# A down projection of a feed-forward slab: one more pair of output tiles by seven half-size products instead of eight

## What is computed

```python
D_FF_2 = 2816
def conv_ffn(h, w_up, conv_w, conv_b, w_down):
    u = h @ w_up                      # 1024 -> 2 * 2816
    u = lax.conv_general_dilated(u, conv_w[:, None, :], ...) + conv_b   # 3 taps along the tokens
    a, gate = jnp.split(u, 2, axis=-1)
    return (jax.nn.silu(gate) * a) @ w_down   # 2816 -> 1024
```

## Time and profile before

| | |
|---|---|
| median of 3 runs | 3196.84 us (3196.56 to 3198.14) |
| time of the profiled execution | 3196.49 us |
| its span in the trace | 3194.6 us |
| PE busy | 3179.1 us (100%) |
| DVE, ACT, POOL busy | 2049.5 us (64%), 1298.8 us (41%), 503.0 us (16%) |
| granted TensorE clock | 0.999 |

### The profile page before, as it was taken

How to read it: one execution, slowest core, us unless ns; L and a number is a source line. 1 busy time by engine, 2 the same in 40 slices (tenths; PEclk the granted TensorE clock), 3 DMA queues, 4 the chain that set the end, 5 groups by cost and what they waited for, 6 DMA issues and landing times.

```text
span 3194.6 us, 45570 instructions
## 1 busy us (share of the span) xinstructions
PE 3179.1 (100%) x16502; PEld 2681.1 (84%) x16502; DVE 2049.5 (64%) x2876; ACT 1298.8 (41%) x1758; POOL 503.0 (16%) x436
## 2 busy tenths in 40 slices
PE   9999999999999999999999999999999999999998
PEld 7788888889998788888889998768888888888887
DVE  8455567586557455567586555666877744588776
ACT  4433333334443433333334453354443523554433
POOL 2100000123221100000123221052202101322111
PEclk9999999999999999999999999999999999999999
DMA  7256324423333156324423332203233332122332
GB/s 268 67 167 208 125 93 167 142 93 106 100 105 101 58 165 205 130 92 164 146 91 108 99 102 87 86 21 101 97 106 99 105 99 92 47 79 93 105 99 79
DMA packets 100044, 359.31 MB, mean 112 GB/s; under 512 B 11057, under 2 KB 13361, under 8 KB 99761
## 3 DMA queue, kind: packets, MB, share of 16 engines
q1 hardware_dynamic: 98960, 354.08, 33.6%
q0 software_dynamic: 928, 3.17, 0.3%
HBM read 355.11 MB, written 2.10 MB: 112 GB/s over the span
## 4 chain that ended last, share of the span: by engine, by line
PE 94%; DVE 1%; POOLq 1%; issue 1%; ACT 1%; DMA 1%; DVEq 0%; SPq 0%; ACTq 0%; POOL 0%
PE pb L759 21%; PE pb L761 21%; PE pb L760 21%; PE pb L1074 6%; PE pb L1314 3%; PE pb L829 2%; PE pb L831 2%; PE pb L830 2%; PE pb L791 1%; PE pb L792 1%; PE pb L795 1%; PE pb L1182 1%; PE pb L1613 1%; DMA raw<-stream 1%; PE pb L1615 1%
## 5 line engine op out<-in xcount | busy, mean ns | idle before, releaser
L2348 DVE TENSOR_TENSOR lo<-raw,hi 128x1024 fp32r<-128x1024 f32 (+1 forms) x484 | 601.5, 1249 | 320.6 <-ACT hi L1685 294.8
L1685 ACT ACTIVATE hi<-raw 128x1024 fp32r<-128x1024 f32 x484 | 508.5, 1056 | 730.8 <-PE pb L761 436.3
L759 PE MATMUL pb<-yH,hi 128*128 128x512 f32 (+1 forms) x1664 | 644.7, 387 | 0.0
L760 PE MATMUL pb<-yL,hi 128*128 128x512 f32 (+1 forms) x1664 | 644.5, 387 | 0.0
L761 PE MATMUL pb<-yH,lo 128*128 128x512 f32 (+1 forms) x1664 | 644.4, 387 | 0.0
L759 PE MATMUL pb<-hH,hi 128*128 128x512 f32 x1128 | 440.8, 391 | 0.0
L760 PE MATMUL pb<-hL,hi 128*128 128x512 f32 x1128 | 439.3, 389 | 0.0
L761 PE MATMUL pb<-hH,lo 128*128 128x512 f32 x1128 | 439.2, 389 | 0.0
L761 PEld LDWEIGHTS pb<-yH,lo 128*128 128x128 f32 x1664 | 312.6, 188 | 63.7
L760 PEld LDWEIGHTS pb<-yL,hi 128*128 128x128 f32 x1664 | 312.6, 188 | 63.2
L759 PEld LDWEIGHTS pb<-yH,hi 128*128 128x128 f32 x1664 | 312.7, 188 | 63.0
(11 more groups left out here) (537 smaller groups left out, 5550.1 us busy)
## 6 DMA issues: line engine op xcount, KB each, us to landing
raw<-stream SPq DMA_DIRECT2D x648, 512.0 KB, 3.4
yF<-first SPq DMA_DIRECT2D x8, 512.0 KB, 11.9
act<-first SPq DMA_DIRECT2D x8, 512.0 KB, 16.5
x<-xT SPq DMA_DIRECT2D x4, 512.0 KB, 7.0
outT<-act SPq DMA_DIRECT2D x7, 256.0 KB, 2.2
act<-crow POOLq DMA_DIRECT2D x2, 512.0 KB, 5.4
tab<-decay SPq DMA_DIRECT2D x1, 1024.0 KB, 7.7
scr<-ws POOLq DMA_DIRECT2D x2, 256.0 KB, 3.1
```

The lines of the kernel that those rows point to most:

```text
L759: pe.matmul(out, whi, ahi, start=first, stop=False)
L760: pe.matmul(out, whi, alo, start=False, stop=False)
L1685: act.activation(hi[:, s], raw[:, s], ACT.Copy).then_inc(hi_ready, 1)
L2348: dve.tensor_tensor(lo[:, s, 0:width], raw[:, s, 0:width], hi[:, s, 0:width].bitcast(F32), ALU.subtract).then_inc(lo_ready, 1)
```

## The change

Pair 1 (down tiles 2 and 3) of the four stretches is done by seven products too, so that only tiles 0 and 1 are plain. As tiles 0 and 1 alone stand ahead of pair 1, several steps are cut finer or moved:

- The first weight sum goes to a place of its own (`d_first`, in `act3`) instead of over a21, and is rounded by its own ACT and DVE steps (`down_sum_hi`, `down_one_lo`); `down_hi` and `down_lo` of slot s1 now take only the upper half of the tile. The order of the sums is first, e2, e4, e3.
- In pair 1, e2, e4 and e3 are rounded and subtracted one by one, 512 wide each. `down_sum_lo` of e2 waits until e4 is made, since its output lies over e2.
- t1 of the last token pair is made by POOL (`m_first`) while product 7 is still being made, and rounded and subtracted ahead of `multiplied(n - 1)`; t4 is rounded ahead of t2 and t3.
- PE does the product with t4 (`lower_sum`) ahead of the one with the first sum and t1 (`other_sum`).
- The loads into slots 2 and 3 of the second four down tiles now wait for pair 1's sums.

```diff
-FAST_DOWN, DOWN_GROUPS = (0, 1), (2, 3)
+FAST_DOWN, DOWN_GROUPS = (0, 1), (1, 2, 3)
+        d_first = lambda q: act3[:, q]
@@ POOL: down_sums
-                four_sums(d_tile(layer, j) + 2 * g, [e[:, i] for i in range(3)],
-                          5 * (at - 1))
+                pool.wait_ge(p_full, 5 * (at - 1 if g == 3 else at if g == 1 else at - 2))
+                pool.tensor_tensor(one, a21, a22, ALU.add)
+                pool.drain().then_inc(s1_ready, 1)
+                pool.tensor_tensor(e2, one, a11, ALU.subtract)
...
+                pool.tensor_tensor(e4, a12, e2, ALU.subtract)
...
+                pool.tensor_tensor(e3, a11, a21, ALU.subtract)
+                pool.drain().then_inc(w_sums, 1)
@@ POOL: middle_sums
+                    pool.wait_ge(product, made + KT - 1)
+                    pool.tensor_tensor(t1, b1[:, TH[1]], b1[:, TH[0]], ALU.subtract)
+                    pool.drain().then_inc(m_first, 1)
@@ PE: fast_down
-                for group in (range(3), (3,)):
...
+                for s in range(2):
+                    pe.wait_ge(lo_ready, tiles.next())
+                    pe.wait_ge(bank_free, banks.next())
+                for m in range(KT):
+                    w = slice((m % 2 * 4 + m // 2) * P, (m % 2 * 4 + m // 2 + 1) * P)
+                    pe.wait_ge(y_ready, y0 + m + 1)
+                    for s in range(2):
+                        ins = three(pb[:, s], hi[:, s, w], lo[:, s, w], midH[:, m], midL[:, m], m == 0, m == KT - 1)
@@ PE: down_group
-                if g == DOWN_GROUPS[0]:
+                if g == 1:
+                    pe.wait_ge(m_lo, tokens_made - 1)
+                product_of(lower_sum, own(s1, 1), token(4)).then_inc(p_full, 1)
+                pe.wait_ge(e_lo, e_count(layer, j, g) - (3 if g == 1 else 1))
+                product_of(other_sum, own(s1, 0), token(1)).then_inc(tile_done, 1)
+                if g == 1:
                     pe.wait_ge(m_lo, tokens_made)
-                product_of(other_sum, own(s1, 0), token(1)).then_inc(p_full, 1)
-                product_of(lower_sum, own(s1, 1), token(4)).then_inc(tile_done, 1)
-                pe.wait_ge(e_lo, at + 1)
+                pe.wait_ge(e_lo, e_count(layer, j, g) - (2 if g == 1 else 0))
                 pe.wait_ge(x_part, added + 1)
                 product_of(one_sum, summed_w(2), token(2), False).then_inc(p_full, 1)
@@ ACT: end of a slab
+                    if fast:
+                        down_hi(layer, j, 1, 1)
+                        act.wait_ge(m_first, slab + 1)
+                        middle_hi(3, 0, 1)
                     gate(n - 1)
                     first += n
                     if fast:
                         act.wait_ge(m_last, slab + 1)
-                        middle_hi(3)
-                        tick(0)
+                        middle_hi(3, 3)
+                        middle_hi(3, 1, 3)
+                        down_sum_hi(layer, j, 1)
```

More of the change, by code:

```diff
@@ L310, in build @@
         d_product = lambda layer, j: layer * (sum(SLABS) - len(SLABS)) + sum(SLABS[:j]) - j
+        d_middle = lambda layer, j: 56 * LAYERS + 8 + layer * (sum(SLABS) + 12) + sum(SLABS[:j])
         gain2 = sb("gain2", [P, 8])
@@ L382, in build @@
         m_last = sem("m_last")
+        m_first = sem("m_first")
         m_hi = sem("m_hi")
@@ L1281, in fast_down @@
             def fast_down(layer, j, y0):
-                for group in (range(3), (3,)):
[L1284 to L1293, removed]
+                for s in range(2):
[6 more added lines that the diff above has]
+                        ins = three(pb[:, s], hi[:, s, w], lo[:, s, w], midH[:, m], midL[:, m], m == 0, m == KT - 1)
+                        if m == KT - 1:
+                            ins.then_inc(tile_done, 1)
                 for g in DOWN_GROUPS:
@@ L3014, in other_of @@
                 def other_of():
-                    dve.wait_ge(p_full, p + 2)
+                    dve.wait_ge(tile_done, done.next(2))
                     dve.tensor_tensor(x1[:, TH[1]], Y, x1[:, TH[1]], ALU.add).then_inc(x_part, 1)
@@ L3024, in lower_of @@
                 def lower_of():
-                    dve.wait_ge(tile_done, done.next(2))
+                    dve.wait_ge(p_full, p + 2)
                     dve.tensor_tensor(x1[:, TH[0]], Z, x1[:, TH[0]], ALU.add)
@@ L3047, in fast_down, with plain_add @@
             def fast_down(layer, j):
-                tick(0)
-                middle_lo(layer, j, 3)
-                for k in range(RING):
+                def plain_add(k):
                     drained.next()
@@ L3054, in fast_down @@
                     dve.tensor_tensor(x[:, k], pb[:, k], x[:, k], ALU.add).then_inc(bank_free, 1)
-                    if k in (1, 2):
-                        down_lo(layer, j, 2, k - 1)
+                one, other, two, lower, upper, last = x_adds(layer, j, 1)
+                middle_lo(layer, j, 3, 3)
+                down_one_lo(layer, j, 1)
+                middle_lo(layer, j, 3, 1, 3)
+                plain_add(0)
+                one()
+                down_sum_lo(layer, j, 1, 0)
+                plain_add(1)
+                lower()
+                down_sum_lo(layer, j, 1, 2)
+                other()
+                two()
+                down_sum_lo(layer, j, 1, 1)
+                down_lo(layer, j, 2, 0)
+                upper()
+                down_lo(layer, j, 2, 1)
+                last()
                 one, other, two, lower, upper, last = x_adds(layer, j, 2)
+                down_one_lo(layer, j, 2)
+                one()
                 down_sum_lo(layer, j, 2)
-                one()
+                lower()
+                other()
+                two()
                 down_lo(layer, j, 3, 0)
-                other()
-                lower()
-                two()
+                upper()
                 down_lo(layer, j, 3, 1)
-                upper()
                 last()
@@ L3068, in fast_down @@
                 one()
+                down_one_lo(layer, j, 3)
                 down_sum_lo(layer, j, 3)
+                lower()
                 tick(1)
                 other()
-                lower()
                 two()
@@ L3134, in conv_ffn @@
                             ins.then_inc(conv_done, 1)
+                    if fast:
+                        down_lo(layer, j, 1, 1)
+                        middle_lo(layer, j, 3, 0, 1)
                     multiplied(n - 1)
```

77 lines of the change are left out of this document (56 added, 21 removed).

## The result

The changed kernel takes 3201.38 us (median of 22 runs, 3200.88 to 3202.37), the kernel before 3196.89 us beside it (22 runs, 3196.33 to 3198.14): a ratio of 1.0014, 95% interval 1.0008 to 1.0021. It is slower by 4.5 us. That is less than the 0.2% (6.4 us) that I had set as the bound of what can be told, but the interval lies wholly above 1, so with this many runs the slowdown is clear of the noise. The profiled execution took 3201.63 us, its span is 3199.9 us, 5.3 more than before. The forecast was 3202.0 and +5.1.

The account below looks back on a forecast made before the run. PE was taken to bound the kernel, busy 3179.1 of 3194.6 us. Waits of 8.3 us less 3.2 saved gave +5.1: 3201.6 profiled, 3202.0 median; overall range 3193.4 to 3207, the main forecast's own 3198 to 3207.

Parts of the forecast that it names:

- PE's gain, a stretch: PE's work per stretch: a pair takes 10.08 us by seven products against 10.88 plain, saving 0.80 us.
- POOL's t1 on DVE: End of the up part: POOL making t1 stretches DVE's work by 0.6 us, bounds 0 and 0.74.
- last product begins: DVE, end of the up part: last product starts 6.9 us after the first plain matmul, instead of 6.11.
- last product published: End of the up part: last product split and published at 9.05 us, in time for PE's need at 9.52.
- rest of e2 ends: Pair 1 on DVE: ends at 17.4 us, held up by POOL's last sum, wanted at 16.64, so 0.9 late.
- rest of e4 ends: Pair 1 on DVE: ends at 19.15 us, wanted at 18.08 + 0.9, 0.6 late with the product's start-up.
- rest of slot 0 (pair 2) ends: DVE's 1024-wide step for pair 2: ends at 23.1 us, wanted at 22.5, 0.75 late with the start-up.
- waits of the first stretch: PE's four waits in stretch one: 0.9 + 0.6 + 0.75 + 0.45 = 2.7 us.
- second, third, fourth: PE's waits in the later stretches, shifted by when DVE's last product starts: 1.25, 3.1 and 1.25 us.
- Rival 2: POOL's chain of sums gets late for pair 3: 2.5 us more a stretch, +15, 3212 us; 9 in 100.
- all is hidden: Rival 1: PE's waits mostly do not arise, change worth 0 to -3.2 us, 3193.6 to 3196.8; 27 in 100.
- Dearer short products: Rival 3, PE: seven short products cost more than two plain tiles, +19, 3216 us; one in 100.

Follow-up runs that it names:

- e3: Not a run in this text: the last of pair 1's four weight sums made by POOL, forecast to end at 16.85 us after the first plain matmul.
- the kernel with ACT copies: Changed kernel with ACT copies in place of POOL's weight sums for pairs 1 and 2, output wrong: 3193.52 us, ratio to before 0.9989.
- the unused sums: Eight sums nobody reads, put on POOL in the kernel where ACT copies replace pairs 1 and 2's sums: 3198.05 us, ratio to before 1.0003.
- pair 1's sums early: Changed kernel with POOL making pair 1's four weight sums during the up part: 3210.35 us, ratio to before 1.0043.
- pairs 1 and 2 early: Changed kernel with POOL making the weight sums of pairs 1 and 2 during the up part: 3221.45 us, ratio to before 1.0075.

## Why the prediction was right

The sum was +5.1, the stretches gave +4.74, the medians +4.5. That the profiled execution came out within 0.1 us of its forecast (3201.63 against 3201.6) is luck: 0.58 of its +5.14 lies ahead of the first stretch, where the change does nothing. Step by step, times from F in the first stretch:

| step | forecast | measured |
|---|---|---|
| PE's gain, a stretch | 0.80 | 0.81 (41.92 against 41.11, POOL away) |
| POOL's t1 on DVE | 0.6 | 0.58 (1.81 for 1.23) |
| last product begins | 6.9 | 7.03 |
| last product published | 9.05 | 9.00 |
| pair 1's sums end | 16.85 | 16.82 |
| rest of e2 ends | 17.4 | 17.37 |
| rest of e4 ends | 19.15 | 19.07 |
| rest of slot 0 (pair 2) ends | 23.1 | 23.00 |
| pair 2's 1536-wide rest ends | 29.3 | 29.19 |
| waits of the first stretch | 2.7 | 2.62 |
| second, third, fourth | 1.25, 3.1, 1.25 | 1.49, 2.66, 1.14 |

(For "published", 6.9 and the 1.97 that the three steps take in the earlier trace rows make 8.87, not 9.05; the later start made up for the slip.) The mechanism is the one forecast, and the steps of the first stretch lie within 0.15 us of where they were put, from turns read in two pairs of rows and carried through some twenty instructions by hand. Four smaller steps failed.

- *"rest of e4 at 19.15, wanted at 18.08 + 0.9: 0.6 late".* The size is right (0.58) and the releaser wrong. 19.15 against 18.98 is only 0.17. PE waits for the add of other_sum, which stands behind that rest on DVE and ends 0.34 later, at 19.41 (2300.44 + 0.41). The terms as written (0.17 and a start-up of 0.1) give 0.27 and not 0.6: an instruction was left out of the text, and the right size does not speak for the working shown.
- *The third stretch, "so e2 is 1.3 late: 3.1".* The start was to be 0.36 later than in the first. It was 0.05 later (7.08 against 7.03), so e2 came 0.96 late and the stretch waited 2.66. The offsets between stretches of before did not carry over.
- *The second stretch, "e4 is late by less than 0.1".* The last product began at 5.89, only 1.14 ahead of the first stretch, not 1.5, and e4 was 0.42 late. In the fourth it was 0.06.
- *Rival 2, "each stretch loses 2.5 us more, in all +15: 3212".* By its own terms the rest would be there at 41 against 39.5, 1.5 late, which gives some +11. Nothing hangs on it, as no wait stood at pair 3.

The second and third cancel in part: 0.44 too much in the third, 0.24 too little in the second.

The rivals: that all is hidden fell with the four waits. That POOL's chain gets late for pair 3 did not come: pair 3's sums were made 31.8 us behind F in the first stretch (31.9 forecast), and no wait stands there. Dearer short products are excluded by the 41.11 us of the kernel with ACT copies.

## What to carry to other kernels

A scheme that trades PE's time for weight sums is paid on the two engines that make them, and where those take turns, in both at once: add their times for the window between the last input and the first use, instead of asking whether each is 60% idle. Moving such sums to an earlier part of the program helps only if DVE has idle time there; here it had none, and the moves cost 9 and 20 us on top of the change. Where two engines take turns, walk the order of both before choosing an edit: holding one engine back alone cost 1.2 us of waits, moving one add alone gave nothing, holding back with a new order gave 4 us. A load put in to stand for real work must have its durations too: the unused sums here were a fifth shorter than the real ones, and brought back half of the waits.

## What the runs showed of the hardware

The turns are exact enough to be calculated with: a `tensor_tensor` of DVE with both inputs in SBUF that meets a POOL sum ends its own duration less 0.13 behind the sum's end (the convolution steps of 0.75: 0.54 behind it), and a sum of 1.29 us that meets it ends 1.14 to 1.16 us behind the DVE step's end; adds from PSUM and ACT's steps show nothing of it.

Long waits of PE sometimes cost twice. With pair 1's sums early, PE waited 3.2 us in the third stretch, and then (windows as above: the wait, the 10.8 us behind it, the next 10):

```profile
2931.00:2934.20 3.20, 0.19 (x1) 0.00 (x0) 2.89 (x6) 0.63 (x1) 0.00 (x0) 1.00 0.35 120
2934.20:2945.00 10.80, 10.75 (x70) 10.12 (x71) 9.77 (x14) 7.96 (x12) 5.68 (x4) 0.84 0.04 14
2945.00:2955.00 10.00, 10.00 (x86) 10.00 (x85) 8.31 (x12) 0.65 (x2) 6.71 (x4) 1.00 0.34 105
```

The granted clock falls to 0.84 as a mean behind the wait, with starts 0.43 us apart for 512 columns in the slow part (the 1.2 GHz level) against 0.2267. With pairs 1 and 2 early, where the waits for the last product took 3.4 to 4.1 us, it fell in all four stretches. In the third it was at 0.50 in the wait itself: starts were 0.43 apart from 2938.7 on already, some matmuls behind an earlier wait of 1.9 us. The rows of that stretch (the wait, the 7.6 us behind it):

```profile
2939.80:2943.40 3.60, 0.39 (x1) 0.00 (x0) 3.24 (x6) 0.63 (x1) 0.00 (x0) 0.50 0.36 100
2943.40:2951.00 7.60, 7.59 (x37) 7.01 (x38) 5.22 (x10) 6.07 (x10) 0.00 (x0) 0.64 0.05 22
```

In the first stretch of the kernel with pair 1 early a wait of the same length (3.23 us) was followed by no fall. Why one and not the other stays open. The waits of under 1 us that the change itself brings left the clock at 1.00 in all four stretches.
